# State-space layer: one root and inverse for the four norm groups, spread by a selector product; first two output tiles multiplied group by group

## What is computed

```
y = y + d_skip * xs                                  # y: (T, 2048), per head
y = y * silu(z)
yg = y.reshape(B, T, 4, 512)                         # four norm groups
yg = yg * rsqrt(mean(yg * yg, axis=-1) + EPS)        # one root per token and group
y = (yg.reshape(B, T, 2048) * norm_g)
out = y @ w_out                                      # 2048 -> 1024
s_new = chunk_decay * s + B^T (decay * x)            # the state that is returned
```

## Time and profile before

| | us |
|---|---|
| median of 3 runs | 1989.22 |
| the 3 runs | 1987.37, 1998.58, 1989.22 |
| the profiled execution | 1987.67 |
| its span, first to last instruction | 1985.9 |
| PE busy in the span | 1852.8 (93%) |
| DVE busy | 1466.5 (74%) |
| ACT busy | 1244.4 (63%) |
| POOL busy | 186.1 (9%) |

### The profile page before, as it was taken

How to read it: one execution, slowest core, us unless ns; L and a number is a source line. 1 busy time by engine, 2 the same in 40 slices (tenths; PEclk the granted TensorE clock), 3 DMA queues, 4 the chain that set the end, 5 groups by cost and what they waited for, 6 DMA issues and landing times.

```text
span 1985.9 us, 31992 instructions
## 1 busy us (share of the span) xinstructions
PE 1852.8 (93%) x10920; PEld 1596.0 (80%) x10920; DVE 1466.5 (74%) x1764; ACT 1244.4 (63%) x1603; POOL 186.1 (9%) x227
## 2 busy tenths in 40 slices
PE   6998989999899997998599999999999999999994
PEld 6997869999799776887388888888888888888883
DVE  7588446663588568433499898988988889898884
ACT  6575245443475254312487888878888787877873
POOL 3021111000134510101100000000000000000001
PEclk9999989999899998998799999999999999999997
DMA  7647588754443931556399999999999999999993
GB/s 264 233 130 244 216 326 339 269 166 149 160 135 130 340 109 44 197 212 238 115 401 371 385 356 377 372 360 391 360 375 372 362 389 364 385 358 371 379 371 142
DMA packets 151104, 558.73 MB, mean 281 GB/s; under 512 B 16496, under 2 KB 16496, under 8 KB 149568
## 3 DMA queue, kind: packets, MB, share of 16 engines
q1 hardware_dynamic: 139248, 508.58, 69.2%
q10 hardware_dynamic: 6832, 28.44, 3.5%
q0 software_dynamic: 4896, 20.18, 2.7%
HBM read 520.61 MB, written 36.52 MB: 281 GB/s over the span
## 4 chain that ended last, share of the span: by engine, by line
PE 80%; issue 7%; DVE 7%; DMA 3%; ACT 2%; POOL 1%; POOLq 0%; SPq 0%; ACTq 0%; DVEq 0%
PE ps L1728 24%; PE ps L1730 24%; PE ps L1729 24%; DVE w_lo L1106 2%; PE ps L2143 1%; PE ps L2028 1%; DMA raw<-in_stream 1%; PE ps L1827 1%; PE ps L1858 1%; POOL rt L2187 1%; PE ps L1874 1%; DMA y_rows<-ye 1%; PE ps L1759 1%; ACT w_hi L700 1%; PE ps L1849 0%
## 5 line engine op out<-in xcount | busy, mean ns | idle before, releaser
L1629 DVE TENSOR_TENSOR w_lo<-raw,w_hi 128x1024 fp32r<-128x1024 f32 x672 | 786.5, 1219 | 49.4 <-ACT w_hi L1036 47.7
L1036 ACT ACTIVATE w_hi<-raw 128x1024 fp32r<-128x1024 f32 x672 | 704.5, 1060 | 139.6 <-PE ps L1730 123.7
L1728 PE MATMUL ps<-w_hi,xe_hi 128*128 128x512 f32 x896 | 358.2, 400 | 4.7 <-DVE w_lo L1629 4.7
L1730 PE MATMUL ps<-w_hi,xe_lo 128*128 128x512 f32 x896 | 354.5, 396 | 0.0
L1729 PE MATMUL ps<-w_lo,xe_hi 128*128 128x512 f32 x896 | 354.0, 395 | 0.0
L700 ACT ACTIVATE w_hi<-raw 128x1024 fp32r<-128x1024 f32 x212 | 220.5, 1050 | 166.3 <-PE ps L1730 116.8
L1106 DVE TENSOR_TENSOR w_lo<-raw,w_hi 128x1024 fp32r<-128x1024 f32 x212 | 266.3, 1269 | 69.6 <-ACT w_hi L700 69.1
L1728 PE MATMUL ps<-h_hi,w_hi 128*128 128x288 f32 x928 | 280.0, 302 | 11.2 <-DVE w_lo L1106 6.8
L1729 PE MATMUL ps<-h_lo,w_hi 128*128 128x288 f32 x928 | 275.8, 297 | 0.0
L1730 PE MATMUL ps<-h_hi,w_lo 128*128 128x288 f32 x928 | 274.9, 296 | 0.0
L1728 PEld LDWEIGHTS ps<-w_hi,xe_hi 128*128 128x128 f32 x896 | 168.9, 189 | 43.1 <-DVE w_lo L1629 5.1
(11 more groups left out here) (396 smaller groups left out, 2550.8 us busy)
## 6 DMA issues: line engine op xcount, KB each, us to landing
raw<-in_experts SPq DMA_DIRECT2D x672, 512.0 KB, 5.5
raw<-in_stream SPq DMA_DIRECT2D x261, 512.0 KB, 4.5
rest<-in_stream SPq DMA_DIRECT2D x28, 512.0 KB, 10.6
x_rows<-zeros ACTq DMA_DIRECT2D x1, 13824.0 KB, 58.9
out_ssd_s<-s_new ACTq DMA_DIRECT2D x16, 512.0 KB, 7.0
xs<-x_rows POOLq DMA_DIRECT2D x9, 512.0 KB, 4.7
y_rows<-ye POOLq DMA_DIRECT2D x9, 512.0 KB, 7.4
out_k<-kmem ACTq DMA_DIRECT2D x2, 1024.0 KB, 7.4
```

What stands on the lines that cost most here:

```text
L1036: act.activation(w_hi[:, (NSPLIT + p) % HL, :], raw[:, slot, :], ACT.Copy) \
L1629: dve.tensor_tensor(w_lo[:, (NSPLIT + p) % HL, :], raw[:, (NRING + p) % RAW, :], w_hi[:, (NSPLIT + p) % HL, :].bitcast(F32), ALU.subtract) \
L1728: pe.matmul(out, l_hi, r_hi, start=start, stop=False)
L1730: return pe.matmul(out, l_lo, r_hi, start=False, stop=stop)
```

## The change

The four groups' sums of squares go into one PSUM bank, each on its own 32 partitions (the all-ones matrix cut to 32 columns), the first three groups interleaved and the fourth behind them. One root (ACT) and one reciprocal (DVE) treat all four at once. A new constant `first`, a 128 x 128 matrix with ones in the rows 0, 32, 64 and 96, then serves as a selector: for each group a matmul over that group's 32 partitions puts its inverse on all 128 partitions of a PSUM bank of its own (`("gn all", g)`). DVE multiplies `y` by the gain and by that bank. The four state matmuls of the second half of the prompt move behind these selector products on PE (`carried(1)`), and the four state additions on DVE move behind all of the normalisation. POOL's multiplication of `s_a` waits in addition for the last gate multiplication (`yz_done`). The first two output tiles are opened together: for each norm group PE multiplies four blocks for tile 0 and four for tile 1; both tiles complete with the last group. Tiles 2 to 7 are as before.

```diff
@@ -81,7 +81,7 @@
                   ("dt_b", 32), ("a_log", 32), ("router", 64), ("w_dt", 256),
                   ("ident", 128), ("tri", 128), ("tri_s", 32), ("last", 128), ("last_s", 32),
                   ("is_last", 8), ("in_seq", 8), ("ones", 128), ("before", 128),
-                  ("lower", 64), ("ebase", 8), ("eps", 1)]:
+                  ("lower", 64), ("ebase", 8), ("eps", 1), ("first", 128)]:
     SMALL[_name] = (_at, _n)
     _at += _n
 NSMALL = _at
@@ -167,8 +167,10 @@
                 p += [(("ab", t, hb), "act", 0)] + [(("state ab", hb), "act", 0)] * (t == 1)
             if hb >= 2:
                 p += [(("y", t, hb - 2), "dve", 0)]
-        p += [(("state", t, g), "act" if t == 0 else "dve", 0) for g in range(GROUPS)]
-    p += [(("gn", g), "act", 0) for g in range(GROUPS)]
+        if t == 0:
+            p += [(("state", t, g), "act", 0) for g in range(GROUPS)]
+    p += [("gn", "act", 0)] + [(("gn all", g), "dve", 0) for g in range(GROUPS)]
+    p += [(("state", 1, g), "dve", 0) for g in range(GROUPS)]
     p += [(("ssd out", j), "dve", 2) for j in range(KD)]
     p += attention(1)
     p += [(("norm", 5), "act", 0), ("logits t", "act", 0), ("logits", "dve", 0)]
@@ -390,8 +392,8 @@
         ysq = at("ysq", [KI, NT], F32, S[6])
         y_hi = at("y_hi", [KI, NT], F32R, S[6])
         y_lo = at("y_lo", [KI, NT], F32R, S[3])
-        grt = at("grt", [GROUPS, NT], F32, S[9])
-        grs = at("grs", [GROUPS, NT], F32, S[9] + GROUPS * NT * 4)
+        grt = at("grt", [NT], F32, S[10])
+        grs = at("grs", [NT], F32, S[10] + NT * 4)
 
         htok = at("htok", [3, D], F32, S[3])
         o_e = S[3] + 3 * D * 4
@@ -514,6 +516,7 @@
         sn_dec = sem("sn_dec")
         sn_done = sem("sn_done")
         yz_done = sem("yz_done")
+        grs_done = sem("grs_done")
         state_out = [sem(f"state_out{i}") for i in range(5)]
         ysq_done = sem("ysq_done")
         msk_done = sem("msk_done")
@@ -997,10 +1000,8 @@
                         act.activation(s_a[:, g * 512:(g + 1) * 512], b, ACT.Copy).then_inc(act_freed, 1)
             square_tiles(6)
             square_tiles(7)
-            for g in range(GROUPS):
-                b = ready(("gn", g), NT)
-                act.activation(grt[:, g, :], b, ACT.Sqrt, bias=eps[:, 0:1], scale=GROUPS / DI) \
-                    .then_inc(act_freed, 1)
+            b = ready("gn", NT)
+            act.activation(grt[:, :], b, ACT.Sqrt, bias=eps[:, 0:1], scale=GROUPS / DI).then_inc(act_freed, 1)
             for g in range(GROUPS):
                 act.wait_ge(y_done, KD + g + 1)
                 act.activation(y_hi[:, 4 * g:4 * g + 4, :], y[:, 4 * g:4 * g + 4, :], ACT.Copy) \
@@ -1544,28 +1545,29 @@
                             tiles = slice(2 * hb - 2, 2 * hb)
                             dve.tensor_tensor(y[:, tiles, :], y[:, tiles, :], zs[:, tiles, :], ALU.mult) \
                                 .then_inc(yz_done, 1)
-                if tt == 1:
-                    dve.wait_ge(state_out[2], 16 * (NB // 2))
-                    dve.wait_ge(state_out[3], 16 * (NB // 2))
-                    dve.wait_ge(sad_done, 1)
-                    for g in range(GROUPS):
-                        b = ready(("state", 1, g))
-                        dve.tensor_tensor(s_b[:, g * 512:(g + 1) * 512], s_a[:, g * 512:(g + 1) * 512], b,
-                                          ALU.add).then_inc(sb_done, 1)
-                        dve.engine_nop().then_inc(dve_freed, 1)
-
+            act_read("gn")
+            dve.reciprocal(grs[:, :], grt[:, :]).then_inc(grs_done, 1)
             for g in range(GROUPS + 1):
                 if g < GROUPS:
-                    act_read(("gn", g))
-                    link(dve.reciprocal(grs[:, g, :], grt[:, g, :]))
+                    b = ready(("gn all", g), NT)
                     for i in range(4 * g, 4 * g + 4):
                         a = dve.scalar_tensor_tensor(y[:, i, :], y[:, i, :], par("ssd_g")[:, i:i + 1],
-                                                     grs[:, g, :], ALU.mult, ALU.mult)
+                                                     b, ALU.mult, ALU.mult)
                     a.then_inc(y_done, 1)
+                    dve.wait_ge(y_done, KD + g + 1)
+                    dve.engine_nop().then_inc(dve_freed, 1)
                 if g:
                     tiles = slice(4 * g - 4, 4 * g)
                     dve.wait_ge(yh_done, KD + g)
                     lo_half(y_lo[:, tiles, :], y[:, tiles, :], y_hi[:, tiles, :], yl_done)
+            dve.wait_ge(state_out[2], 16 * (NB // 2))
+            dve.wait_ge(state_out[3], 16 * (NB // 2))
+            dve.wait_ge(sad_done, 1)
+            for g in range(GROUPS):
+                b = ready(("state", 1, g))
+                dve.tensor_tensor(s_b[:, g * 512:(g + 1) * 512], s_a[:, g * 512:(g + 1) * 512], b,
+                                  ALU.add).then_inc(sb_done, 1)
+                dve.engine_nop().then_inc(dve_freed, 1)
             residual(("ssd out",), gains("g_mem", 1), 6 * KD)
             attention(1)
 
@@ -2000,6 +2002,14 @@
                 for g, qd in enumerate(quads):
                     out = open_group(("s state", b, g))
                     close(pe.matmul(out, btm4[qd, b, :], xd4[qd, :], start=True, stop=True))
+            def carried(tt):
+                pe.wait_ge(act_freed, FREED[KEY["bt", tt]][1])
+                pe.wait_ge(xd_done, tt + 1)
+                for g in range(GROUPS):
+                    out = open_group(("state", tt, g))
+                    close(pe.matmul(out, bt[:, g * P:(g + 1) * P], xd[:, g * 512:(g + 1) * 512],
+                                    start=True, stop=True))
+
             for tt, (c0, n) in enumerate(TOK[:2]):
                 if tt:
                     token_major(1)
@@ -2060,22 +2070,37 @@
                             a = pe.matmul(o, s_a[:, hd * 64:(hd + 1) * 64], ce[:, j * n:(j + 1) * n],
                                           start=False, stop=True)
                     close(a)
-                pe.wait_ge(act_freed, FREED[KEY["bt", tt]][1])
-                pe.wait_ge(xd_done, tt + 1)
-                for g in range(GROUPS):
-                    out = open_group(("state", tt, g))
-                    close(pe.matmul(out, bt[:, g * P:(g + 1) * P], xd[:, g * 512:(g + 1) * 512],
-                                    start=True, stop=True))
+                if tt == 0:
+                    carried(0)
+            out = open_group("gn", NT)
+            for gs in ((0, 1, 2), (3,)):
+                pe.wait_ge(ysq_done, 2 * gs[-1] + 2)
+                for k in range(4):
+                    for g in gs:
+                        a = pe.matmul(out[quads[g], :], ones[:, 0:32], ysq[:, 4 * g + k, :],
+                                      start=(k == 0), stop=(k == 3))
+            close(a)
+            outs = [open_group(("gn all", g), NT) for g in range(GROUPS)]
+            pe.wait_ge(grs_done, 1)
+            for g, qd in enumerate(quads):
+                close(pe.matmul(outs[g], par("first")[qd, :], grs[qd, :], start=True, stop=True))
+            carried(1)
+
+            k0 = NEED[KEY["ssd out", 0]] - 2
+            outs = [open_group(("ssd out", j), NT) for j in range(2)]
             for g in range(GROUPS):
-                out = open_group(("gn", g), NT)
-                pe.wait_ge(ysq_done, 2 * g + 2)
-                for k in range(4):
-                    a = pe.matmul(out, ones, ysq[:, 4 * g + k, :], start=(k == 0), stop=(k == 3))
-                close(a)
-            for j in range(KD):
+                pe.wait_ge(yl_done, KD + g + 1)
+                for j in range(2):
+                    for k in range(4 * g, 4 * g + 4):
+                        hi, lo = weights(k0 + 2 * j + k // 8)
+                        cols = slice(k % 8 * P, (k % 8 + 1) * P)
+                        a = mm3(outs[j], hi[:, cols], lo[:, cols], y_hi[:, k, :], y_lo[:, k, :],
+                                k == 0, k == KI - 1)
+                    if g == GROUPS - 1:
+                        close(a)
+            for j in range(2, KD):
                 k0 = NEED[KEY["ssd out", j]] - 2
-                product(("ssd out", j), [(k0 + k // 8, k % 8, k) for k in range(KI)], y_hi, y_lo, NT,
-                        yl_done if j == 0 else None, KD, 4)
+                product(("ssd out", j), [(k0 + k // 8, k % 8, k) for k in range(KI)], y_hi, y_lo)
             attention(1)
             norm(("norm", 5), 5)
             few("logits", par("router"), NE)
@@ -2293,6 +2318,7 @@
                 if tt == 1:
                     pool.wait_ge(dec_done, 2)
                     pool.wait_ge(full, KEY["y", 1, 7] + 1)
+                    pool.wait_ge(yz_done, KI // 2)
                     sv = s_a[:, :].rearrange("p (h f) -> p h f", f=64)
                     pool.tensor_tensor(sv, sv, cdec[:, :].unsqueeze(2).broadcast_to([P, HEADS, 64]),
                                        ALU.mult).then_inc(sad_done, 1)
@@ -2396,6 +2422,7 @@
```

(1 more changed line is left out.)

## The result

| | before | after |
|---|---|---|
| median, 20 runs each (us) | 1996.57 | 1981.95 |
| lowest and highest | 1983.71, 2000.94 | 1973.08, 1991.41 |
| ratio after/before | | 0.9946, 95% interval 0.9927 to 0.9965 |
| the profiled execution | 1987.67 | 1987.40 |

What follows compares the result with a forecast made beforehand. PE, busy 93%, was taken as the bound, so only its waits, here for DVE's normalisation chain, could shrink. The eighth tile moves from 835.7 to 823.3, 12.4 us, less 0.5 and 0.2: 11.7; forecast 1976.5, range 1971.5 to 1984.

Steps and rivals of the forecast that it cites:

- The stage: Normalisation and output tiles: the eighth tile ends at 823.3 instead of 835.7, 12.4 us less.
- steps: DVE chain behind the reciprocal: each next group's multiplications and low half take 3.2 us, where a group cost 5.0.
- The quarters of the array: Narrow sums of squares run beside each other, first three groups in 2.0 us; rival that they do not: 1979.5, chance 0.04.
- Reading the inverse from PSUM: DVE multiplications of y: 1.8 us a group, same as from SBUF; the skill's surcharge would add 0.26 us each.
- the additions of tiles 0 and 1: Sign in the profile after: the first two residual additions come together at about 785.
- the stand of the profiled time to the median: Whole kernel: median of the runs shown taken as 1.5 us above the profiled 1987.67; forecast 1976.5.
- The rival on the clock: PE's stops at 763.2 to 765.8 and 770.6 to 771.8 lower the clock: gain 8.7 to 10.4 us, chance 0.16.
- POOL's wait: Last gate multiplication on DVE no longer meets POOL: 0.76 us instead of 3.71, ending 2.95 us earlier.
- The state matmuls: Behind the selectors, 3.70 us with 1.2 us cover left; at low clock up to 7.2 us; 0.5 us taken off.
- The pair: First two output tiles: a quarter takes 3.2 us, as long as DVE's step, both done at 784.8 without PE waits.
- Given back later: Rival: attention transfers behind the stage set the pace, half the gain lost, 6 us left, 1983; chance 0.12.
- slower: Rival: clock stays at 0.50 from the first quarter on; all eight tiles low cost 41 us, 2016; chance 0.03.

Runs made afterwards that it cites:

- The fills: Kernels with two or three unread f32 matmuls of 512 columns where PE waits for the first masked product; medians 1988.14 (unchanged kernel), 1977.44, 1977.28, 1975.97 us.
- lo_late: Changed kernel with four low halves of weights made only behind the first half of the prompt; 12 runs, median 1975.54 us, ratio 0.9927 to the kernel before.
- after: First profiled execution of the changed kernel, no further edit: 1987.40 us, stage 65.7 us.
- before_again: Second profiled execution of the kernel before, no edit: 1998.28 us, stage 74.2 us.
- pool_only: Kernel before with only POOL's multiplication of the carried state waiting for the last gate multiplication; one execution, stage 75.1 us.
- no_pair: Changed kernel with the output tiles one after the other as before; one execution, stage 68.1 us.
- state_first: Changed kernel with the state's four matmuls and four additions back ahead of the sums of squares and the reciprocal; one execution, stage 70.3 us.
- before: First profiled execution of the kernel before, without the change: 1987.67 us, stage 76.9 us.
- after_again: Second profiled execution of the changed kernel, no further edit: 1977.20 us, stage 64.5 us.
- pair_only: Kernel before with only the first two output tiles multiplied together, norm group by norm group; one execution, stage 70.9 us.
- no_pool_wait: Changed kernel without POOL's wait for the last gate multiplication; one execution, stage 70.6 us.
- before_fill: Kernel before with three unread f32 matmuls where PE waits for the first masked product; 12 runs, median 1988.14 us, ratio 0.9979.
- lo_late_fill: Changed kernel with late low halves of weights and two unread matmuls in PE's wait; 6 runs, median 1975.97 us, ratio 0.9924 to the kernel before.

## Why the prediction was right or wrong, point by point

**The stage: right against the profile that it was worked out from.** Its sum was 12.4 us, 76.9 to 64.5. The two executions of the changed kernel took 65.7 and 64.5. In the lower group that is 12.4 us in the stage (76.9 and 64.5) and 12.0 in the total; in the upper it is 8.5 in the stage (74.2 and 65.7), since there the kernel before runs fewer of its tiles at the low clock. The length of that low stretch was taken from one execution. In the second every step is where the sum had it, counted from the stage's start (predicted, measured): reciprocal 5.0, 5.0; first multiplication 7.8, 7.8; first low half finished 13.0, 12.8; steps 3.2, 3.1. The quarters of the array do run beside each other (4.40 us for all sums, predicted 4.4, where 16 full-width ones took 7.92). Reading the inverse from PSUM costs nothing: eight multiplications in 3.61 us, where four from SBUF took 1.80; the surcharge that the Trainium skill ("Perfetto Trace Analysis", Optimizing Scalar/DVE Operations) would have here is not seen. Two slips change nothing: 1.80 us for 1152 columns makes 0.25 us for 160 columns, not 0.17, and a multiplication would be 0.51 us by that (0.45 measured); and 1976.5 is 2.8 us, not 2, below the 1979.3 of the least change. A small miss: the additions of tiles 0 and 1 do not come together; tile 0 is complete 1.6 us before tile 1, half a quarter, and its addition stands 4.0 us before the other (794.2 and 798.2).

**The step that failed: the stand of the profiled time to the median.** The sum was set on 1987.67, "the median of the runs shown is 1.5 us above the profiled one". The three runs shown were 1987.37, 1989.22 and 1998.58, and the sum uses their median and nothing of their spread. 1998.58 was one of the larger of two groups: in 20 runs the median is 1996.57, 8.9 us above the profiled execution and not 1.5. For the changed kernel the same: 1975.6 in its lower group, 0.9 us below the forecast, and 1981.95 over all. That 1976.5 lies near a time that the kernel does take is due to the sum; which share of the runs takes it, the prediction had no term for. The rival on the clock named only PE's waits inside the stage. The wait that goes with the group lies 50 us ahead. There DVE makes four low halves of weights before the first mask; the changed kernel's rows:

```profile
701.31 4.62 DVE L1107 TENSOR_TENSOR w_lo<-raw,w_hi 128x1024 fp32r<-128x1024 f32 x4
...
707.89 1.12 PE L2067 MATMUL ps<-mt,xt 128*64 128x128 f32 x8 [2.25 <-DVE mt L1518]
```

PE waits 2.25 us, the clock goes to 0.50, and the following eight steps, with PE busy for 17.9 of the 18 us from 711 to 729, do not bring it back; it is full again at 734, in the state's matmuls of the first half. The fills show that work on PE in that wait is enough to keep it up; the low halves may be a part of the wait's cause, not all of it (`lo_late`).

The wait itself is not the same in the two groups, and the first difference lies further ahead. In the nine profiles of kernels without a fill and with the old low halves, PE waits 2.25 or 2.26 us for the first mask in the five that have the low stretch (`after`, `before_again`, `pool_only`, `no_pair`, `state_first`), and 0.17 to 0.66 us in the four that have not (`before`, `after_again`, `pair_only`, `no_pool_wait`). In these four the clock had been at 0.50 for 3.4 to 6.8 us between 697 and 706, so PE came later to the same place; in the five it was at 1.00 from 694.2 at the latest until the wait. Before, then changed, both first profiles, then PE's arrival in the second profile of the changed kernel:

```profile
700.00:703.00 3.00, 3.00 (x15) 1.77 (x10) 1.97 (x4) 0.00 (x0) 0.50 (x1) 0.50 0.91 360
```

```profile
700.00:703.00 3.00, 3.00 (x30) 3.00 (x28) 3.00 (x5) 1.07 (x2) 1.29 (x1) 1.00 0.75 289
```

```profile
708.12 0.66 PE L2067 MATMUL ps<-mt,xt 128*64 128x128 f32 x8 [0.17 <-DVE mt L1518]
```

The mask comes at about the same time in both (707.06 and 707.29 in the two profiles of the changed kernel); it is PE that comes early in one and late in the other. So in these profiles a short low stretch just ahead spares the long one, by making the wait short. That the fill holds the clock by itself is seen in `before_fill` and `lo_late_fill`, which had no low stretch from 690 on and stayed at 1.00. What puts the clock at one level or the other at 700, and why the eight steps hold whichever level they begin with, was not tested and stays open.

**POOL's wait: right in the whole, wrong as a term.** 2.95 us were put down to it alone. `pool_only` shows the reciprocal 0.9 us later, not 2.95 earlier: DVE waits for POOL's product instead. The 2.95 us belong to it and the move of the additions together (`no_pool_wait` shows them, 2.9 us), and for the gate multiplication the prediction gave that move no part.

**The state matmuls: the cover was just too short.** They ran at the low clock (6.15 and 5.40 us instead of 3.70). In the first profile they ended at 783.0, 1.1 us behind the first low half, in the second 0.3 us behind it; the first product of the tiles started 0.5 and 0.3 us behind that low half. 0.5 us had been taken off for it.

**The pair: a smaller share than I gave it later.** Nothing in the sum separates it; the 6.4 us, a whole tile, stand in what I expected of `no_pair`. Its worth behind short steps is 2.4 to 3.6 us.

**Given back later, slower:** neither came. Behind the stage the last addition keeps its distance to the end within 1.3 us: 1985.7 - 834.2 = 1151.5 us after, 1985.9 - 835.7 = 1150.2 before; in the second profiles 1153.5 and 1153.2.

## What to carry to other kernels

Before a sum of 12 us is set on one profiled execution, look at how the single runs lie, not only at their median: three runs with one 11 us off may be two groups, and then both the median and the profile stand for one of them by chance. When two executions differ, go back to the first time at which they part; here the long clock stretch 50 us ahead of the change was itself the outcome of a shorter one before it. A wait that is taken away from one instruction is only won if nothing behind it on the same engine waits for the work that was pushed back.

## What the runs showed of the hardware

The same instructions can run for 27 us (706.7 to 734) at either granted clock: with PE busy for 9.00 of 9 us, 90 records at 1.00 or 50 at 0.50. In nine profiles the low one followed a PE wait of 2.25 us (five), the full one a wait of 0.17 to 0.66 us (four). With 1.9 to 2.8 us of full-width f32 matmuls in that wait, into a bank about to be overwritten, the clock was 1.00 in all four profiles and none of 33 runs was in the upper group. A DVE multiplication of two SBUF operands that met POOL's 3.62 us instruction took 3.7 us instead of 0.76 (3.71 in the kernel before, 3.70 in `no_pool_wait`). Two DVE instructions with an operand in PSUM, started at 758.90 in the kernel before and beside POOL from 759.00 on, took their usual 0.60 us together.
